# Two GpSimd waits and the low parts of one weight slot moved within a chunked gated delta rule on one Trainium2 core

## The chip, the cores and the metric

The kernel runs on one core of one Trainium2 chip. The metric is the device time of one execution in microseconds (us), taken as the median over several executions. Five engines work side by side and meet at semaphores: TensorE (PE in the profile, its weight loads as PEld), VectorE (DVE), ScalarE (ACT), GpSimd (POOL) and SyncE (SP), which only issues DMAs here. Each engine runs its own instructions strictly in the order in which they stand. TensorE writes to the accumulator memory PSUM, in eight banks that the kernel hands out in rotation.

## The reference

Two transformer blocks run one after the other on 256 tokens of width 1024. The first is a hybrid of neighbourhood attention and a gated delta rule, each over eight heads of 64; the second has two layers of feed-forward, token mixing, gating and feed-forward. The change lies inside the delta rule of the first block:

```python
def _gdn_chunked(q, k, v, g, beta, s0):
    gc = jnp.cumsum(g, axis=-1)
    decay = jnp.exp(jnp.where(incl, gc[..., :, None] - gc[..., None, :], -jnp.inf))
    kb = k * beta[..., None]
    lower = jnp.where(strict, jnp.einsum('bnhid,bnhjd->bnhij', kb, k) * decay, 0.0)
    a_mat = lower + jnp.eye(C, dtype=f32)
    rhs = jnp.concatenate([v * beta[..., None], kb * jnp.exp(gc)[..., None]], axis=-1)
    sol = lax.linalg.triangular_solve(a_mat, rhs, left_side=True, lower=True, unit_diagonal=True)
    ...
    def step(S, xs):
        v_new = u_i - jnp.einsum('bhck,bhkv->bhcv', w_i, S)
        o_i = jnp.einsum('bhck,bhkv->bhcv', qd_i, S) + jnp.einsum('bhij,bhjv->bhiv', qk_i, v_new)
        S = S * gt_i[..., None, None] + jnp.einsum('bhck,bhcv->bhkv', kd_i, v_new)
        return S, o_i
```

It runs forward and backward over context and latent tokens. After it come the neighbourhood attention, the merge of both branches, and the second block, whose output is returned. All of it is in float32. The kernel gets that precision out of rounded matmuls by splitting each weight in a rounded high part and the low part that is left, and each activation likewise, and summing three products.

## The kernel before, in words

**Weights.** Weights stream from HBM in slots of 128x2048 into a ring of four. For each split slot ScalarE makes the high part in two halves (`head`, recorded at line 1341) and VectorE subtracts it for the low part, in two halves of 128x1024 (`part`, recorded at line 1792; both its operands lie in SBUF, in `ring` and `w_hi_first`). Each half raises `w_lo_done` by one. The first block has SPLIT_1 = 25 split slots, numbered 0 to 24. The last eight of them carry the weights of four gate blocks, two slots each: slots 23 and 24 belong to the last, `g1_3`. TensorE's `gate_blocks` does eight steps for each, of six products of 128x512; steps 0 to 3 use slot 23 and steps 4 to 7 use slot 24.

**The delta rule.** The 512 tokens are four tiles of 128, and a round n = 0 to 3 handles one tile in each direction d = 0, 1. One round is this ladder:

- `lower(n)` (VectorE): the strictly triangular matrix of a round, products out of PSUM times the decays `Et`. This is read one round ahead: round 0's loop does `lower(1)`. Four instructions, which empty four PSUM banks that TensorE wants back.
- `coefficients(n)` and `invert(n)` (VectorE): shuffles, then a 16x16 inverse by elimination, 30 small products and subtractions, each waiting for the one ahead of it. All are of the tile `cst` with two operands in SBUF.
- `spread(n)` (VectorE): lays the small inverses out for TensorE, four products and two transposes. The transposes raise the semaphore `X32`, by two in a round, to eight after round 3. They are the "first-level inverses", at line 2050.
- first, second and last level (TensorE, with ScalarE copies and `first_level(n)` of VectorE between them): the inverse grows from 16 to 32, 64 and 128.
- `VN`, `SU`, `PO` (TensorE): new values, state update, output. `VN` needs the right side `R` (VectorE, line 1786) and the last copies of the inverse by ScalarE (line 1562).
- `state(n)` (VectorE): the state `sblk` is scaled and added to. In round 0 it is a copy.

In round 0, TensorE puts the gate block `g1_3` between the levels: two steps, first level out, two steps, second level in, two steps, second level out, two steps, then the queries' transposes (line 418).

**GpSimd** works down one list. `mul` of it is recorded at line 1248:

- `scaled(n)`: for each direction `gm`, of 128x1024, which TensorE's `decays(n)` reads, and `kb`, of 128x512, which its `scaled_keys(n)` reads. The title calls these the coefficients.
- `decayed_keys(n)`: two products of 128x512.
- `masked_decays(n)`: two of 128x1024 on `Et`, which VectorE's `KQ` products read in rounds 2 and 3.
- the bias masks: two of 128x2048 on `ring` (line 1305), which the attention reads.

Its second DMA of `x_in` stands between `decayed_keys(2)` and `masked_decays(3)`.

**What sets the order.** The program is written out by hand for each engine. There is no scheduler. PSUM banks rotate in TensorE's order of opening: `open_bank` waits until the group eight openings earlier was read out. So the first-level output of round 0 (`Z4`) waits for the first two instructions of `lower(1)`, and `KQ` of direction 1 in round 3 for the two `QS` groups that VectorE reads after `R`.

Of the kernel before, what the change touches and what calls it, by code (L numbers as in the profile page):

```python
# [73 lines left out]
SPLIT_1 = 6 + 1 + 18  # L74
# [5 lines left out]
def build(nc, stream, const, const_2, par1, par2, ln_params, rpb_bands, x_in, ctx_in, positions, out):  # L80
# [8 lines left out]
    with ctx:  # L89
# [5 lines left out]
        def S(name):  # L95

            if name not in sems:
                sems[name] = ctx.enter_context(nc.semaphore(name))
            return sems[name]
# [76 lines left out]
        X32 = [carve(Z + 13312 + 768 * d, 2, 8, 32) for d in range(2)]  # L176
# [198 lines left out]
        def lo_sem(j):  # L375
            return S("w_lo_done"), 2 * j
# [864 lines left out]
        @block.gpsimd  # L1241
        def _(pool):
            pool.dma_start(xtok, x_in.rearrange("(t p) f -> p t f", p=P)).then_inc(S("x_in"), 16)
            pool.dma_start(ctxtok, ctx_in.rearrange("(t p) f -> p t f", p=P)).then_inc(S("ctx_in"), 16)
            pool.dma_start(cst[:, 0:CONST_FIRST], const).then_inc(S("const_in"), 16)
            pool.dma_start(pos_i[:, :], positions).then_inc(S("pos_in"), 16)
            pool.wait_ge(S("const_in"), 16)
            mul = lambda o, a, b: nc.gpsimd.tensor_tensor(o, a, b, ALU.mult)
            pool.wait_ge(S("g_ready"), 1)
            pool.wait_ge(S("qk_ready"), 1)  # L1250
            pool.wait_ge(S("beta"), 1)
            pool.wait_ge(S("na_ready"), 1)
            summed(pool, ("dnz", 1))
            def keys(t):
                return dntok[:, t, 512:1024].rearrange("p (h e) -> p h e", e=64)

            def scaled(n):
                for d in range(2):
                    t = ORDER[d][n]
                    if n:  # L1260
                        for half in range(2):
                            summed(pool, ("Et", n - 1, d, half))
                        summed(pool, ("kbT", n - 1, d))
                    mask = K("lower") if d == 0 else K("upper")
                    mul(gm[d][:, :, :], lg[:, t, d * 8:d * 8 + 8].unsqueeze(2).to_broadcast([P, 8, P]),
                        mask.unsqueeze(1).to_broadcast([P, 8, P])).then_inc(S("gm"), 1)
                    mul(kb[d].rearrange("p (h e) -> p h e", e=64), keys(t),
                        beta[:, t, d * 8:d * 8 + 8].unsqueeze(2).to_broadcast([P, 8, 64])).then_inc(S("kb"), 1)

            def decayed_keys(n):  # L1270
                for d in range(2):
                    t = ORDER[d][n]
                    if n:
                        summed(pool, ("SU", n - 1, d))
                    mul(kdec[d].rearrange("p (h e) -> p h e", e=64), keys(t),
                        egc[:, t, 16 + d * 8:24 + d * 8].unsqueeze(2).to_broadcast([P, 8, 64])).then_inc(S("kdec"), 1)

            def masked_decays(n):
                for d in range(2):
                    for half in range(2):  # L1280
                        moved(pool, ("KK", n, d, half))
                    incl = K("upper_incl") if d == 0 else K("lower_incl")
                    mul(Et[n % 2][d], Et[n % 2][d], incl.unsqueeze(1).to_broadcast([P, 8, P])).then_inc(S("Etm"), 1)

            scaled(0)
            scaled(1)
            pool.wait_ge(S("X32"), 2)
            scaled(2)
            moved(pool, "gc")
            summed(pool, ("g1_3", 1))  # L1290
            for d in range(2):
                nc.gpsimd.memset(Xt[d], 0.0).then_inc(S("zeros"), 1)
            decayed_keys(0)
            scaled(3)
            decayed_keys(1)
            masked_decays(2)
            decayed_keys(2)
            for d in range(2):
                summed(pool, ("Y6", 2, d))
            pool.dma_start(xtok, x_in.rearrange("(t p) f -> p t f", p=P)).then_inc(S("x_in"), 16)  # L1300
            masked_decays(3)
            pool.wait_ge(S("bias_in"), 16 * 4)
            for t in range(2):
                b64 = bias[t].rearrange("p h (y c) -> p (h y) c", c=64)
                nc.gpsimd.tensor_tensor(b64, b64, K("na_mask").unsqueeze(1).to_broadcast([P, 32, 64]), ALU.add)\
                    .then_inc(S("bias"), 1)

            def ln_load(L, which):

                pool.dma_start(lnp, ln_params[L, (which - 1) * 2 * D:which * 2 * D].rearrange("(a b) -> a b", b=D)  # L1310
                               .partition_broadcast(P)).then_inc(S("ln_in"), 16)

            for L in range(LAYERS):
                if L:
                    pool.wait_ge(S(f"x{L}0"), 2)
                else:
                    pool.wait_ge(S("x00"), 4)
                    pool.dma_start(cst[:, CONST_COMMON:CONST_COLS], const_2).then_inc(S("const2_in"), 16)
                pool.dma_start(pr2, par2[L, :, :]).then_inc(S(f"par{L}_in"), 16)
                ln_load(L, 1)  # L1320
                for which in (1, 2):
                    pool.wait_ge(S(f"x{L}{which}"), 2)
                    ln_load(L, which + 1)
# [448 lines left out]
        def _(dve):  # L1772
# [18 lines left out]
            def sub(o, a, b):  # L1791
                return V_.tensor_tensor(o, a, b, ALU.subtract)  # L1792
# [40 lines left out]
            def part(upto):  # L1833

                while parted[0] < upto:
                    j = parted[0]
                    at = SPLIT_SLOTS[j] % RING * SLOT
                    hi, lo = parts(j)
                    for i in range(2):
                        h = slice(i * SLOT // 2, (i + 1) * SLOT // 2)  # L1840
                        dve.wait_ge(S("w_hi_done"), 2 * j + i + 1)
                        sub(lo[:, h], ring[:, at + h.start:at + h.stop], hi[:, h].bitcast(f32))\
                            .then_inc(S("w_lo_done"), 1)
                    parted[0] += 1
# [247 lines left out]
            part(23)  # L2092
            invert(0)
            spread(0)
            part(SPLIT_1)
            for n in range(4):
                if n:
                    state(n - 1)
                if n < 3:
                    lower(n + 1)  # L2100
                first_level(n)
                if n < 3:
                    coefficients(n + 1)
                if n == 0:
                    invert(n + 1)
                    summed(dve, ("g1_3", 1))
                for d in range(2):
                    t = ORDER[d][n]
                    v = heads(dntok[:, t, 1024:1536])
                    R = heads(Rr[d])  # L2110
                    bt = wide(beta[:, t, d * 8:d * 8 + 8], 64)
                    cum = wide(egc[:, t, d * 8:d * 8 + 8], 64)
                    if n:
                        ps, free = take(dve, ("KS", n, d))
                        mul(R, heads(ps), cum).then_inc(free, 1)
                        moved(dve, ("KS", n, d))
                        link(sub(R, v, R))
                        mul(R, R, bt).then_inc(S("R"), 1)
                    else:
                        mul(R, v, bt).then_inc(S("R"), 1)  # L2120
                for d in range(2):
                    t = ORDER[d][n]
                    cum = wide(egc[:, t, d * 8:d * 8 + 8], 64)
                    if t < 2:
                        ps, free = take(dve, ("QS", n, d))
                        if n == 2:
                            mul(heads(odn[:, t, :]), heads(ps), cum).then_inc(free, 1)
                        else:
                            mul(heads(dtmp), heads(ps), cum).then_inc(free, 1)
                            moved(dve, ("QS", n, d))  # L2130
                            link(add(odn[:, t, :], odn[:, t, :], dtmp))
                for d in range(2):
                    if ORDER[d][n] < 2:
                        dve.wait_ge(S("Etm"), 2 * (n - 2) + d + 1)
                        halves("KQ", n, d, lambda h, ps: mul(Et[n % 2][d][:, h, :], Et[n % 2][d][:, h, :], ps), True)
                if n in (1, 2):
                    invert(n + 1)
                if n < 3:
                    spread(n + 1)
# [515 lines left out]
```

## Time and profile before

| | |
|---|---|
| median of 3 runs | 1771.11 us (1769.55 to 1786.57) |
| the profiled execution | 1768.32 us |
| its span, first to last instruction | 1766.5 us |
| TensorE busy | 1690.6 us, 96% |
| VectorE busy | 1087.7 us, 62% |
| ScalarE busy | 832.1 us, 47% |
| GpSimd busy | 62.3 us, 4% |
| DMA | 285.75 MB, 162 GB/s |
| TensorE on the chain that ended last | 85% of the span |

All times on the timeline are counted from the first instruction of the profiled execution. TensorE's instructions are pipelined, so a busy time is not a time at its peak; its idle times are exact to a few tenths. The profile puts each idle time down to the instruction whose semaphore came last. The granted clock is a share of full speed: 1.00 is 2.4 GHz and 0.50 is 1.2 GHz.

### The profile page before, as it was taken

To read this page: it belongs to the slowest core of one execution; us is meant where nothing else is said; L and a number is where in the kernel's file an instruction comes from. 1 tells how busy PE (TensorE), PEld (TensorE's weight loads), DVE (VectorE), ACT (ScalarE), POOL (GpSimd) and SP (SyncE) were. 2 spreads that over 40 slices of the span, in tenths; PEclk is the share of its full clock that TensorE was granted. 3 is DMA by queue.
4 is the path that set the end of the run, shared out by engine and by line. 5 is a ranking of instruction groups with operands and counts; after the bars stand their busy time and mean duration, and the time that the engine had idled before them with its cause. 6 is when DMAs were issued, how large, how long until landed. Compare 5 with 4: busy or idle time off the path is not lost.

```text
span 1766.5 us, 24089 instructions
## 1 busy us (share of the span) xinstructions
PE 1690.6 (96%) x9832; PEld 1369.1 (78%) x9832; DVE 1087.7 (62%) x1602; ACT 832.1 (47%) x1224; POOL 62.3 (4%) x48
## 2 busy tenths in 40 slices
PE   7999989778999999999999999999999999999998
PEld 2778877677558887887888888788887878888886
DVE  3689576976236556655786554655556547875555
ACT  3444565534135444454645444444435546454442
POOL 0000133020000000000000000000000000000000
PEclk9999998887999999999999999999999999999999
DMA  8333421010365555543445555565555534455553
GB/s 350 143 122 118 167 73 26 4 72 1 143 235 185 188 191 191 190 168 119 167 167 214 191 180 183 203 216 190 183 176 206 174 140 147 164 217 191 178 182 117
DMA packets 41518, 285.75 MB, mean 162 GB/s; under 512 B 4416, under 2 KB 6592, under 8 KB 8000
## 3 DMA queue, kind: packets, MB, share of 16 engines
q1 hardware_dynamic: 39120, 268.61, 42.9%
q0 software_dynamic: 2288, 15.60, 2.3%
q8 instruction: 79, 1.29, 0.3%
q14 instruction: 31, 0.25, 0.0%
HBM read 283.14 MB, written 1.05 MB: 161 GB/s over the span
## 4 chain that ended last, share of the span: by engine, by line
PE 85%; DVE 7%; ACT 3%; DMA 2%; issue 2%; SPq 0%; POOL 0%; DVEq 0%; ACTq 0%; POOLq 0%
PE psum L415 82%; PE psum L418 3%; DMA ring<-stream 2%; DVE ring_lo L1792 2%; DVE cst L1786 1%; DVE arena L1786 1%; ACT arena L1341 1%; ACT cst L1341 1%; DMA arena<-stream 1%; ACT w_hi L1341 1%; DVE cst L1792 0%; DVE cst L2017 0%; ACT L1607 0%; DVE arena L2251 0%; DVE sblk L1855 0%
## 5 line engine op out<-in xcount | busy, mean ns | idle before, releaser
L1792 DVE TENSOR_TENSOR ring_lo<-ring,w_hi 128x1024 fp32r<-128x1024 f32 x416 | 489.1, 1222 | 237.4 <-ACT w_hi L1341 236.1
L1341 ACT ACTIVATE w_hi<-ring 128x1024 fp32r<-128x1024 f32 x416 | 415.4, 1053 | 296.8 <-DMA ring<-stream 228.5
L415 PE MATMUL psum<-w_hi,xT_hi 128*128 128x512 f32 (+1 forms) x1184 | 465.9, 393 | 12.9 <-DVE xT_lo L1792 12.2
L415 PE MATMUL psum<-w_hi,xT_lo 128*128 128x512 f32 (+1 forms) x1184 | 460.7, 389 | 0.0
L415 PE MATMUL psum<-ring_lo,xT_hi 128*128 128x512 f32 (+1 forms) x1184 | 460.6, 389 | 0.0
L415 PEld LDWEIGHTS psum<-w_hi,xT_hi 128*128 128x128 f32 x1184 | 224.2, 189 | 58.9 <-issue 14.8
L415 PEld LDWEIGHTS psum<-w_hi,xT_lo 128*128 128x128 f32 x1184 | 224.2, 189 | 46.2
L415 PEld LDWEIGHTS psum<-ring_lo,xT_hi 128*128 128x128 f32 x1184 | 224.2, 189 | 43.6
L1786 DVE TENSOR_TENSOR arena<-psum,arena 128x256 f32<-128x256 f32 (+1 forms) x144 | 73.9, 520 | 175.3 <-ACT arena L1618 124.3
L1341 ACT ACTIVATE arena<-psum 128x512 f32<-128x512 f32 (+6 forms) x165 | 87.0, 556 | 199.0 <-PE psum L415 141.5
L415 PE MATMUL psum<-arena 32*32 32x32 f32 (+7 forms) x2088 | 144.9, 259 | 33.5 <-ACT arena L1562 7.0
L415 PEld LDWEIGHTS psum<-arena 32*32 32x32 f32 (+3 forms) x2088 | 130.4, 161 | 48.3 <-issue 34.1
L415 PE MATMUL psum<-w_hi,hfT_hi 128*128 128x512 f32 x352 | 137.9, 392 | 0.0
L415 PE MATMUL psum<-w_hi,hfT_lo 128*128 128x512 f32 x352 | 137.2, 390 | 0.0
L415 PE MATMUL psum<-ring_lo,hfT_hi 128*128 128x512 f32 x352 | 137.2, 390 | 0.0
L1618 ACT ACTIVATE arena<-psum 128x256 f32<-128x256 f32 x88 | 33.7, 384 | 167.2 <-PE psum L415 167.2
L418 PE MATMUL psum<-cst,arena 128*128 128x128 f32 (+1 forms) x676 | 96.4, 279 | 4.3 <-ACT arena L1586 1.7
L418 PEld LDWEIGHTS psum<-cst,arena 128*128 128x128 f32 (+1 forms) x676 | 80.8, 143 | 22.7 <-issue 5.9
L1792 DVE TENSOR_TENSOR ring_lo<-ring,w_hi_first 128x1024 fp32r<-128x1024 f32 x50 | 65.1, 1348 | 21.8 <-ACT w_hi_first L1341 21.7
L415 PEld LDWEIGHTS psum<-w_hi,hfT_lo 128*128 128x128 f32 x352 | 66.1, 188 | 13.7
L415 PEld LDWEIGHTS psum<-w_hi,hfT_hi 128*128 128x128 f32 x352 | 66.1, 188 | 13.5
L415 PEld LDWEIGHTS psum<-ring_lo,hfT_hi 128*128 128x128 f32 x352 | 66.1, 188 | 13.5
(245 smaller groups left out, 1819.8 us busy)
## 6 DMA issues: line engine op xcount, KB each, us to landing
ring<-stream SPq DMA_DIRECT2D x249, 1024.0 KB, 4.8
arena<-ln_params POOLq DMA_DIRECT2D x6, 1024.0 KB, 5.8
arena<-par POOLq DMA_DIRECT2D x2, 1858.0 KB, 9.5
arena<-stream SPq DMA_DIRECT2D x3, 1024.0 KB, 6.9
arena<-x_in POOLq DMA_DIRECT2D x2, 1024.0 KB, 9.1
ring<-rpb_bands SPq DMA_DIRECT2D x4, 512.0 KB, 6.1
cst<-const POOLq DMA_DIRECT2D x1, 1728.0 KB, 7.6
arena<-ctx_in POOLq DMA_DIRECT2D x1, 1024.0 KB, 19.3
```

Of the source, the lines that this page charges most:

```text
L415: owe(nc.tensor.matmul(o, lhsT, rhs, start=first, stop=last), sem)
L418: owe(nc.tensor.transpose(o, i, ident), sem)
L1341: return A(o, i, ACT.Copy)
L1618: A(hs[:, cb % 2, t, :], ps[:, 0:256], ACT.Silu).then_inc(S(f"silu{L}{f}"), 1)
L1786: return V_.tensor_tensor(o, a, b, ALU.mult)
L1792: return V_.tensor_tensor(o, a, b, ALU.subtract)
```

## The change

Three edits. GpSimd's `scaled(2)` waits for `w_lo_done` at 48, which is both halves of slot 23, in place of `X32` at 2. Its `masked_decays(3)`, and with it the bias masks that follow, waits in addition for `X32` at 8, the end of `spread(3)`. VectorE makes only slot 23's low parts after `spread(0)`; those of slot 24 stand behind `first_level(0)`, ahead of `coefficients(1)`.

```diff
@@ gpsimd
             scaled(0)
             scaled(1)
-            pool.wait_ge(S("X32"), 2)
+            lo, count = lo_sem(23)
+            pool.wait_ge(lo, count + 2)
             scaled(2)
             moved(pool, "gc")
             summed(pool, ("g1_3", 1))
@@ gpsimd
             for d in range(2):
                 summed(pool, ("Y6", 2, d))
             pool.dma_start(xtok, x_in.rearrange("(t p) f -> p t f", p=P)).then_inc(S("x_in"), 16)
+            pool.wait_ge(S("X32"), 8)
             masked_decays(3)
             pool.wait_ge(S("bias_in"), 16 * 4)
@@ vector
             part(23)
             invert(0)
             spread(0)
-            part(SPLIT_1)
+            part(SPLIT_1 - 1)
             for n in range(4):
                 if n:
                     state(n - 1)
                 if n < 3:
                     lower(n + 1)
                 first_level(n)
+                part(SPLIT_1)
                 if n < 3:
                     coefficients(n + 1)
```

VectorE at the end of `spread(0)`, before. The second row is the transposes of `spread(0)`, `ring_lo` rows are low parts of a slot (two halves each; the buffer numbered 54 holds slot 23, the one numbered 56 slot 24), `ring<-psum,arena` is `lower(1)`, `arena<-arena,psum` and the transposes behind it are `first_level(0)`, and the last row opens `coefficients(1)`.

```order
L1786 TENSOR_TENSOR arena<-cst 128x256 x4
L2050 STREAM_TRANSPOSE arena<-arena 128x256 x2
L1792 TENSOR_TENSOR ring_lo<-ring,w_hi_first_54 128x1024 x2
L1792 TENSOR_TENSOR ring_lo<-ring,w_hi_first_56 128x1024 x2
L1786 TENSOR_TENSOR ring<-psum,arena 128x4x128 x4
L1792 TENSOR_TENSOR arena<-arena,psum 128x256 x2
L2062 STREAM_TRANSPOSE arena<-arena 128x256 x2
L2005 STREAM_TRANSPOSE cst<-cst 128x256 x2
```

The same place of the changed kernel, whose lines of VectorE have numbers two higher:

```order
L1788 TENSOR_TENSOR arena<-cst 128x256 x4
L2052 STREAM_TRANSPOSE arena<-arena 128x256 x2
L1794 TENSOR_TENSOR ring_lo<-ring,w_hi_first_54 128x1024 x2
L1788 TENSOR_TENSOR ring<-psum,arena 128x4x128 x4
L1794 TENSOR_TENSOR arena<-arena,psum 128x256 x2
L2064 STREAM_TRANSPOSE arena<-arena 128x256 x2
L1794 TENSOR_TENSOR ring_lo<-ring,w_hi_first_56 128x1024 x2
L2007 STREAM_TRANSPOSE cst<-cst 128x256 x2
```

The two subtractions of slot 24 moved past `lower(1)` and `first_level(0)`, six instructions and two transposes.

GpSimd from `decayed_keys(2)` to the bias masks, before: two products of keys, the DMA of `x_in`, `masked_decays(3)`, and the masks at line 1305.

```order
L1248 TENSOR_TENSOR arena<-arena,small 128x512 [waits bank1_full]
L1248 TENSOR_TENSOR arena<-arena,small 128x512 [waits bank2_full]
L1300 DMA arena<-x_in 128x2x1024 [waits bank0_full,bank7_full]
L1248 TENSOR_TENSOR arena<-arena,cst 128x1024 [waits bank6_empty,bank5_empty]
L1248 TENSOR_TENSOR arena<-arena,cst 128x1024 [waits bank0_empty,bank7_empty]
L1305 TENSOR_TENSOR ring<-ring,cst 128x2048 [waits bias_in]
L1305 TENSOR_TENSOR ring<-ring,cst 128x2048
```

And in the changed kernel:

```order
L1248 TENSOR_TENSOR arena<-arena,small 128x512 [waits bank1_full]
L1248 TENSOR_TENSOR arena<-arena,small 128x512 [waits bank2_full]
L1301 DMA arena<-x_in 128x2x1024 [waits bank0_full,bank7_full]
L1248 TENSOR_TENSOR arena<-arena,cst 128x1024 [waits bank6_empty,bank5_empty,X32]
L1248 TENSOR_TENSOR arena<-arena,cst 128x1024 [waits bank0_empty,bank7_empty]
L1307 TENSOR_TENSOR ring<-ring,cst 128x2048 [waits bias_in]
L1307 TENSOR_TENSOR ring<-ring,cst 128x2048
```

No row moved here; the fourth gained the wait for `X32`, and three stand behind it.

## Rows read from the trace of the kernel before

**Rows 1.** Windows of the span: busy us (instructions) by engine, granted clock, DMA share, GB/s.

```profile
250.00:392.00 142.00, 109.83 (x2479) 100.31 (x2481) 117.88 (x266) 67.74 (x152) 42.09 (x23) 0.83 0.11 26
...
512.00:1766.50 1254.50, 1230.29 (x5730) 1018.56 (x5728) 756.75 (x964) 599.19 (x816) 4.54 (x9) 0.99 0.51 182
```

**Rows 2.** Whom TensorE waited for between 252 and 400 us: total, times, longest.

```profile
PE psum L415 <- DVE arena L2050: 6.5, 2, 6.2
PE psum L415 <- DVE ring L1786: 5.9, 1, 5.9
```

**Rows 3.** Timeline of GpSimd: start, us, instruction, count, idle before and its releaser.

```profile
252.52 2.94 POOL L1248 TENSOR_TENSOR arena<-small,cst 128x1024 f32<-128x1024 f32 x1 [26.54 <-DVE arena L2050]
...
279.26 2.49 POOL L1248 TENSOR_TENSOR arena<-arena,small 128x512 f32<-128x512 f32 x2
285.98 1.89 POOL L1248 TENSOR_TENSOR arena<-small,cst 128x1024 f32<-128x1024 f32 x1 [4.23 <-PE psum L418]
287.83 1.04 POOL L1248 TENSOR_TENSOR arena<-arena,small 128x512 f32<-128x512 f32 x1
...
351.11 0.77 POOL L1300 DMA_DIRECT2D arena<-x_in  x1 [21.96 <-PE psum L415]
351.90 4.66 POOL L1248 TENSOR_TENSOR arena<-arena,cst 128x1024 f32<-128x1024 f32 x2
356.52 7.58 POOL L1305 TENSOR_TENSOR ring<-ring,cst 128x2048 f32<-128x2048 f32 x2
```

**Rows 4.** Timeline of VectorE, from an earlier slot's low parts to round 0's end.

```profile
217.23 2.36 DVE L1792 TENSOR_TENSOR ring_lo<-ring,w_hi_first 128x1024 fp32r<-128x1024 f32 x2 [0.69 <-ACT w_hi_first L1341]
...
252.48 8.88 DVE L1792 TENSOR_TENSOR ring_lo<-ring,w_hi_first 128x1024 fp32r<-128x1024 f32 x4
261.28 2.47 DVE L1786 TENSOR_TENSOR ring<-psum,arena 128x512 f32<-128x512 f32 x4
...
266.18 0.77 DVE L2005 STREAM_TRANSPOSE cst<-cst 128x256 f32<-128x256 f32 x2 [0.16 <-ACT cst L1341]
...
270.60 0.29 DVE L2023 COPY cst<-cst 128x256 f32<-128x256 f32 x1
...
279.68 2.62 DVE L1786 TENSOR_TENSOR arena<-arena,small 128x512 f32<-128x512 f32 x2
```

**Rows 5.** Timeline of TensorE around the gate block and the first `VN`.

```profile
262.70 0.27 PE L415 MATMUL psum<-arena 32*32 32x32 f32 x3 [5.87 <-DVE ring L1786]
...
277.34 1.34 PE L418 MATMUL psum<-cst,arena 128*128 128x128 f32 x8
...
289.50 1.30 PE L415 MATMUL psum<-arena 128*128 128x64 f32 x5 [3.26 <-ACT arena L1562]
```

**Rows 6.** Windows of low granted clock, columns as in rows 1.

```profile
262.00:269.00 7.00, 6.30 (x139) 5.33 (x140) 5.97 (x17) 4.98 (x12) 0.26 (x1) 0.51 0.01 2
290.00:300.00 10.00, 10.00 (x64) 9.88 (x67) 4.37 (x8) 2.16 (x4) 3.13 (x3) 0.52 0.01 2
```

**Rows 7.** Timeline of VectorE around the last inverse and the state of round 2.

```profile
351.40 12.80 DVE L1786 TENSOR_TENSOR cst<-cst 128x52 f32<-128x52 f32 x1
364.24 0.25 DVE L1792 TENSOR_TENSOR cst<-cst 128x52 f32<-128x52 f32 x1
...
373.74 0.42 DVE L1786 TENSOR_TENSOR sblk<-sblk,small 64x256 f32<-64x256 f32 x1
...
378.04 0.69 DVE L1789 TENSOR_TENSOR arena<-arena,psum 128x512 f32<-128x512 f32 x1
...
381.10 0.69 DVE L1786 TENSOR_TENSOR arena<-psum,small 128x512 f32<-128x512 f32 x1 [0.60 <-PE psum L415]
...
386.66 0.69 DVE L1786 TENSOR_TENSOR arena<-psum,small 128x512 f32<-128x512 f32 x1
```

**Rows 8.** Timeline of TensorE at the last first level and its last `KQ`.

```profile
373.76 0.47 PE L415 MATMUL psum<-arena 32*32 32x32 f32 x17 [6.24 <-DVE arena L2050]
...
387.49 0.72 PE L415 MATMUL psum<-arena 64*128 64x128 f32 x8 [0.53 <-DVE arena L1786]
```

## The prediction

> **What bounds the kernel now.** I read the windows first, to see where TensorE is not the bound. From 512 us on it is busy 1230.29 of 1254.50 us with the clock at 0.99 [rows 1]: nothing before that stretch can change it, except its start. From 250 to 392 us it is busy for only 109.83 of 142 us, at a mean clock of 0.83, while VectorE is busy for 117.88 and the DMAs for 11% [rows 1]. That is the delta rule, and all three edits lie in it. A time won there moves the rest forward unless a wait inside the delta rule takes it back. Then I read whom TensorE waits for there. Two single waits belong to the edits: 5.87 us for `lower(1)` at 262.70 and 6.24 us for `spread(3)` at 373.76 [rows 2, 5, 8]. Last come the timelines of GpSimd and VectorE, to see why those two are late.
>
> Both are late in the same way. A half of low parts takes 1.18 us with GpSimd at rest (2.36 for two [rows 4]), but the four at 252.48 take 8.88, 2.22 each, while `scaled(2)` runs beside them [rows 3, 4]. GpSimd's first product there takes 2.94 against 1.89 for the same product at 285.98 [rows 3]. The two take turns, one instruction each. At 351.40 it is worse: a product of `invert(3)` of a kind that takes 0.25 us takes 12.80, and ends when GpSimd's four products, 4.66 + 7.58 = 12.24 us, are done [rows 3, 7]. `lower(1)`, which reads one operand from PSUM, keeps 2.47 us for four though GpSimd is still busy for its first microsecond [rows 3, 4]. So I take it that only VectorE's instructions with two SBUF operands are held.
>
> **Site A, the two edits around `scaled(2)`.** Now slot 23's low parts run alone, 252.48 to 254.84, and `lower(1)` follows to 257.31; its first two instructions, all that TensorE's `Z4` needs, are out by 256.1. TensorE is then still in its gate steps until 256.83 (262.70 less 5.87 [rows 5]), so the wait of 5.87 goes whole. The clock falls with it: after that wait TensorE ran at 0.51 for 7 us with 6.30 busy [rows 6]. At full clock this is some 3.2 us less. No pause of such length stands ahead of it any more, so the queries' transposes at 277.34 [rows 5] come 9.0 us sooner, at 268.3.
>
> Is slot 24 late for TensorE? `Z4` starts at 256.8, and `first_level(0)`, done 3.3 us after `Z4`'s start before (to 266.0, the start of the next row less its wait [rows 4, 5]), is done 2.7 us after it at full clock, at 259.5. `scaled(2)`, 5.86 us alone (twice 1.89 + 1.04 [rows 3]), runs from 254.85 and meets the two halves at its end: they take 3.4 us in place of 2.36, to 262.95, the first by 260.8 to 261.8. TensorE wants them at about 261.4 and 265.3 (eight gate steps and the levels between them, at the full-clock pace). Cost 0 to 0.4 us; I take 0.
>
> Who is late next? `VN` of round 0, at 289.50, waited 3.26 us for ScalarE [rows 5], whose chain starts at the gate block's end and therefore moves by 9.0 too, to 280.5. It also needs `R`. VectorE: 262.95, plus 4.42 for `coefficients(1)` (266.18 to 270.60), plus 9.08 for `invert(1)` (to 279.68 [rows 4]), is 276.45. Before, `invert(1)` had GpSimd beside it only in a memset. Now GpSimd's `decayed_keys(0)`, two products of 1.04, come at 279.26 − 9.0 = 270.3, into the middle of it, and hold it for 2.1: 278.55. And `scaled(3)` comes at 285.98 − 9.0 = 277.0 [rows 3], with 1.5 us of `invert(1)` left, of which 0.8 is three or four two-operand steps. Each lets one GpSimd product by: 5.86 us and four steps of 0.2 bring it to 283.6, two transposes 0.7, the first `R` 0.65: 285.0. So `VN` starts at 285.0, not 280.5, and of the 9.0 us **4.5 remain**. The bounds are 4.5 (all four steps held) and 9.0 (`invert(1)` finds its end before `scaled(3)`; `R` then waits once, to 279.6, in time). I take the lower because all four steps fall within 0.8 us, though a microsecond either way decides it. `spread(1)` stands behind `R` and is ready ten microseconds ahead of TensorE.
>
> **Site B, the masks behind `X32` at 8.** `invert(3)` loses its 12.5 us, save up to 0.2 beside the DMA issue at 351.11 [rows 3, 7]. `spread(3)` ends at 351.7 + (373.74 − 364.24) = 361.2 [rows 7] in the old time, and TensorE, whose own work runs until 367.5 (373.76 less 6.24 [rows 8]), no longer waits. The 12.24 us of GpSimd work now start at 361.3, beside `state(2)`. This has four products with two SBUF operands (`sblk` and `small`). By turns they let the four GpSimd products by: the last ends at 361.3 + 12.24 + 3 × 0.42 + 0.42 = 375.2, and with one addition of 0.42 and one of 0.69 `state(2)` is done at 376.3. Before, it was 378.73 [rows 7]. That is 2.4 us. The 0.34 and 0.60 us that VectorE waited for TensorE behind it go too, since TensorE has done its levels meanwhile. The last reader that TensorE's `KQ` waits for at 387.49, the product at 386.66 [rows 7, 8], thus comes 3.3 us sooner. **I take 3.3.** The ladder behind is TensorE's and ScalarE's, and moves along. The bounds: 1.1, if the first state product is held through all four, as at 351.40 (361.3 + 12.24 + 5.0 for `state(2)` is 378.5; the 0.94 of waits goes); and 5.5, if VectorE is ahead of GpSimd at each turn and the last mask falls behind `state(2)`. The readers of `masked_decays(3)` stand behind the product at 386.66 in VectorE's order [rows 7], those of the masks behind them, and 375 is well ahead of that: nothing.
>
> The Trainium skill, page "SBUF — State Buffer", section "Who interferes with whom", says that a VectorE instruction with two SBUF inputs contends with a GpSimd instruction that reads SBUF, and that whoever issues first has the port for that whole instruction. By that rule one VectorE instruction waits for one of GpSimd's: the 8.88 agrees, and site B gives 3.3. The 12.80 of one instruction beside four does not agree; by it site B gives 1.1.
>
> **The sum.** 1768.32 − 4.5 − 3.3 = 1760.5 us for a run like the profiled one. This stood 2.8 us under the median of the three, so the forecast is **1763 us**.
>
> **The rivals.**
> - *No collision at A* (`invert(1)` ends before `scaled(3)`): 9.0 + 3.3, so 1759. For it: the margin is 1.5 us of a chain that I added up over 26. Chance 0.25.
> - *Held through at B*: 4.5 + 1.1, so 1765. For it: the one long case in the trace, and the same four instructions. Against: at 252.48 they took turns, and at 351.40 a DMA issue of GpSimd was under way. Chance 0.15.
> - *All of it and more*: 9.0 + 5.5, and half of the clock's other low stretches in the delta rule, another 3 to 4: 1753. Chance 0.07.
> - *The change does not reach its wait*: TensorE waits for slot 24 instead of slot 23. The price is at most the 0.4 to 1 us above; the bulk would still go. Chance 0.03, 1764.
> - *Slower.* The pause ahead of the first `VN` grows from 3.26 us to 7.8. After the pause of before, the clock was at 0.52 through 290 to 300 [rows 6], where TensorE was fully busy. If the longer pause drags the low clock through the rest of the round and on into round 1, another 16 us of TensorE's work at half clock costs 8 and eats the gain; 20 cost 10: 1768.32 − 7.8 + 10, with 2.8, is 1773. It decides once low stretches of the delta rule grow by over 16 us in all. For it: the pauses of 5.87 and 3.26 us were both followed by such stretches [rows 5, 6]. Against: one long pause and one low stretch go. Chance 0.05.
>
> The forecast itself has 0.45. **The range** is 1754 to 1771: it holds the first three cases with their bounds and a microsecond or two of run to run; left out are most of the case of 1753 and the slower one. About 1% (18 us) is what counts as a change here. Faster by over 1%, under 1753.4: 0.07. Within 1%: 0.90. Slower by over 1%: 0.03.
>
> **What would show it.** Low parts at 252.48 of 2.36 us for two, and `Z4` at 256.8 with no wait: site A's first half. `VN` of round 0 waiting for VectorE's line of `R` at 285, not for ScalarE at 280.5: the collision; single steps of `invert(1)` of over 1 us beside it. Steps of `invert(3)` all of 0.25; `spread(3)`'s wait gone from TensorE's list; products of `sblk` of 2 to 4 us each (turns), or one of 12. From 512 us on all rows alike, shifted. I am wrong if the queries' transposes move by under 7 us, if `VN` starts within a microsecond of 289.50, or if TensorE's rows behind 512 us lengthen.

## The result

| | before | changed |
|---|---|---|
| median | 1773.32 us (18 runs) | 1760.89 us (18 runs) |
| lowest to highest | 1765.13 to 1786.57 | 1755.76 to 1770.48 |
| profiled execution | 1768.32 us | 1760.34 us |

The ratio is 0.9941, 95% interval 0.9921 to 0.9961: the change makes the kernel faster by 10 us, 7 to 14. A second set of 12 runs gave 0.9939 (0.9916 to 0.9962). The forecast was 1763, in a range of 1754 to 1771.

The windows of the changed kernel, with the borders moved along with the work (columns as in [rows 1]):

```profile
250.00:380.00 130.00, 105.88 (x2460) 96.13 (x2459) 112.86 (x272) 68.25 (x152) 38.79 (x23) 0.87 0.12 27
...
500.00:1758.50 1258.50, 1234.28 (x5727) 1021.14 (x5725) 756.32 (x964) 599.24 (x816) 4.22 (x8) 0.99 0.52 181
```

The border is 12 us earlier because TensorE's last `KQ` comes 11.7 us earlier (375.76 below, 387.49 in [rows 8]). So the delta rule is 12 us shorter, and the rest is 4 us longer; the last section puts that down to the clock. TensorE's waits between 250 and 392 us, to lay beside [rows 2]:

```profile
PE psum L415 <- DVE arena L1788: 8.4, 3, 5.2
PE psum L415 <- ACT arena L1564: 7.0, 4, 3.3
...
PE psum L415 <- DVE arena L2052: 0.3, 1, 0.3
```

The 5.9 us for `lower(1)` are gone from the list and the 6.2 us for `spread(3)` shrank to nothing (the 0.3 are round 0's). A new one of 2.3 us is inside the first line. TensorE's own rows in the changed kernel: its first first-level product of round 0, the start of `Z4`, the second half of `Z4`, the queries' transposes, `VN` of round 0, `VN` of round 2, the last `KQ`, `VN` of round 3.

```profile
254.03 0.36 PE L415 MATMUL psum<-arena 32*32 32x32 f32 x20 [0.29 <-DVE arena L2052]
...
258.31 0.26 PE L415 MATMUL psum<-arena 32*32 32x32 f32 x8
...
259.69 0.18 PE L415 MATMUL psum<-cst,arena 32*32 32x32 f32 x1 [0.64 <-issue]
...
271.20 0.44 PE L418 MATMUL psum<-cst,arena 128*128 128x128 f32 x2
...
283.36 0.41 PE L415 MATMUL psum<-arena 128*128 128x64 f32 x2 [3.26 <-ACT arena L1564]
...
347.69 6.56 PE L415 MATMUL psum<-arena 128*128 128x64 f32 x39 [1.90 <-ACT arena L1564]
...
375.76 0.38 PE L415 MATMUL psum<-arena 64*128 64x128 f32 x2 [2.29 <-DVE arena L1788]
...
383.46 2.75 PE L415 MATMUL psum<-arena 128*128 128x64 f32 x23 [0.82 <-ACT arena L1564]
```

And two of the same places in the kernel before, the first first-level product of round 0 and `VN` of round 2 (the others are in [rows 5, 8]; `VN` of round 3 started at 394.39):

```profile
252.50 1.29 PE L415 MATMUL psum<-arena 32*32 32x32 f32 x128 [0.30 <-DVE arena L2050]
...
355.15 2.08 PE L415 MATMUL psum<-arena 128*128 128x64 f32 x17 [1.90 <-ACT arena L1562]
```

Round 0 began 1.5 us later here than in the trace of before (254.03 against 252.50, ahead of all edits), so I compare intervals. From the first first-level product to `VN` of round 0 it is 29.3 us, where it was 37.0 (289.50 less 252.50). The last `KQ` still waits for VectorE, as [rows 8] had it, but longer: 2.29 us in place of 0.53.

### The profile page after: what moved, and what is told of

Same layout as the page of the kernel before. It is cut to its first block, busy times and chain, and to the rows that moved or that the text cites. A ratio compares the mean times of both kernels' runs of the same rounds, so it can differ in the third digit from the quotient of the medians.

```text
span 1758.5 us, 24089 instructions
## 1 busy us (share of the span) xinstructions
PE 1692.0 (96%) x9832; PEld 1367.2 (78%) x9832; DVE 1081.2 (61%) x1602; ACT 832.6 (47%) x1224; POOL 59.0 (3%) x48
## 3 DMA queue, kind: packets, MB, share of 16 engines
q8 instruction: 79, 1.29, 0.3%
## 4 chain that ended last, share of the span: by engine, by line
PE 87%; DVE 6%; ACT 3%; DMA 2%; issue 1%; SPq 0%; POOL 0%; DVEq 0%; ACTq 0%; POOLq 0%
PE psum L415 84%; PE psum L418 3%; DMA ring<-stream 1%; DVE ring_lo L1794 1%; ACT arena L1343 1%; DVE arena L1788 1%; DVE sblk L1788 1%; ACT cst L1343 1%; DMA arena<-stream 1%; ACT w_hi L1343 1%; DVE cst L2019 0%; ACT L1609 0%; DVE arena L2254 0%; DVE sblk L1857 0%; DVE cst L1794 0%
## 5 line engine op out<-in xcount | busy, mean ns | idle before, releaser
L415 PE MATMUL psum<-arena 32*32 32x32 f32 (+7 forms) x2088 | 141.1, 252 | 23.4 <-DVE arena L1788 8.4
L415 PEld LDWEIGHTS psum<-arena 32*32 32x32 f32 (+3 forms) x2088 | 126.7, 154 | 38.1 <-issue 30.4
L1794 DVE TENSOR_TENSOR ring_lo<-ring,w_hi_first 128x1024 fp32r<-128x1024 f32 x50 | 61.2, 1268 | 21.5 <-ACT w_hi_first L1343 21.4
```

Of the source, the lines that this page charges most:

```text
L415: owe(nc.tensor.matmul(o, lhsT, rhs, start=first, stop=last), sem)
```

## The experiments

Two intervals tell the sites apart better than the whole time does. Site A is from the first first-level product of round 0 to `VN` of round 0. Site B is from `VN` of round 2 to `VN` of round 3. In us, from one trace each:

| kernel | site A | site B |
|---|---|---|
| before | 37.0 | 39.2 |
| changed, two traces | 29.3, 30.0 | 35.8, 35.3 |
| edits 1 and 3 | 29.7 | 40.6 |
| edit 2 | 35.9 | 35.4 |
| edit 3, two traces | 30.0, 30.0 | 39.5, 40.5 |
| edit 1 | 33.1 | 39.2 |
| idle work ahead of `invert(1)` | 35.2 | 36.5 |
| the same, `scaled(3)` behind `R` | 30.7 | 35.3 |
| masks apart, two traces | 31.4, 29.9 | 34.4, 35.6 |
| DMA behind the masks | 36.1 | 38.1 |

Rows that share the code of a site show how far a single trace can be off. Site A with its old code took 37.0, 35.9 and 36.1 us (before, edit 2, DMA behind the masks), and with its new code 29.3, 30.0, 29.7, 31.4 and 29.9: 6.3 us between the means, where the first pair of traces shows 7.7. Site B took 38.1 to 40.6 us in the six traces without edit 2, and 35.3 to 36.5 in the five with it and its masks in place: about 4 us.

### Each site alone

Site A alone (edits 1 and 3):

```diff
-            pool.wait_ge(S("X32"), 2)
+            lo, count = lo_sem(23)
+            pool.wait_ge(lo, count + 2)
...
-            part(SPLIT_1)
+            part(SPLIT_1 - 1)
...
                 first_level(n)
+                part(SPLIT_1)
```

> The first and third edit alone (scaled(2) behind slot 23's low parts, slot 24's behind first_level(0)); masked_decays(3) waits for nothing new. Theory: the two sites add up. From the first first-level product of round 0 to VN of round 0 29.3 us as in the changed kernel (37.0 before), and one product of invert(3) held for about 12 us again, with TensorE waiting 6 us for spread(3). Time 7 to 8 us under before. Rival: the sites are coupled, and most of the gain comes with the masks: under 4 us.

Site B alone (edit 2):

```diff
+            pool.wait_ge(S("X32"), 8)
             masked_decays(3)
```

> The second edit alone (masked_decays(3) and the masks behind X32 at 8). Theory: VN of round 2 to KQ of direction 1 in round 3 takes 28.1 us as in the changed kernel (32.3 before), the four sblk products are held by turns, 2 to 4 us each, and the 5.9 us wait for lower(1) stays. Time 4 us under before. Rival: without site A nothing comes of it: within 1 us.

By the intervals both expectations held. Site A took 29.7 us with edits 1 and 3, and one step of `invert(3)` was held again:

```profile
347.14 12.86 DVE L1793 TENSOR_TENSOR cst<-cst 128x56 f32<-128x56 f32 x1
```

Site B took 35.4 us with edit 2, and `VN` of round 2 to the last `KQ` 28.45 (expected 28.1); the 5.87 us wait for `lower(1)` stayed. One detail was not as expected: three of the four `sblk` products were held there (1.91, 3.50 and 2.74 us), and the fourth took 0.42, since TensorE released the first of them later. So each site keeps its own interval, whatever the code of the other. The whole times came out smaller than expected: ratio 0.9978 (0.9949 to 1.0006) for site A, some 4 us, and 0.9995 (0.9970 to 1.0020) for site B, 1 us. The intervals take in 7 and 4 us, and they take in none; the two sum to half of the 10 us of both together. That the sites are additive is read from the traces and not shown by the times.

### Which edit does site A's work

Edit 3 alone, slot 24's low parts behind `first_level(0)`:

```diff
-            part(SPLIT_1)
+            part(SPLIT_1 - 1)
...
                 first_level(n)
+                part(SPLIT_1)
```

> The third edit alone: slot 24's low parts behind first_level(0), scaled(2) still on X32 at 2, so that it runs beside slot 23's low parts. By turns these take about 4.1 us in place of 2.36, lower(1) starts 1.8 us later, and TensorE waits about 1.5 us for it ahead of Z4, in place of 5.9 before and none in the changed kernel. If the order of VectorE alone did it, the wait is gone; if the sharing alone did it, it stays near 5.

Edit 1 alone, `scaled(2)` behind slot 23:

```diff
-            pool.wait_ge(S("X32"), 2)
+            lo, count = lo_sem(23)
+            pool.wait_ge(lo, count + 2)
```

> The first edit alone: scaled(2) waits for slot 23's low parts, slot 24's still ahead of lower(1). Slot 23's take 2.36 us and slot 24's about 4.2, together 6.6 in place of 8.9, so TensorE waits 3.5 to 3.9 us for lower(1) in place of 5.9.

VectorE with edit 3 alone:

```profile
252.87 4.06 DVE L1792 TENSOR_TENSOR ring_lo<-ring,w_hi_first 128x1024 fp32r<-128x1024 f32 x2
256.86 2.47 DVE L1786 TENSOR_TENSOR ring<-psum,arena 128x512 f32<-128x512 f32 x4
```

and with edit 1 alone:

```profile
253.54 6.33 DVE L1793 TENSOR_TENSOR ring_lo<-ring,w_hi_first 128x1024 fp32r<-128x1024 f32 x4
```

Slot 23's two halves took 4.06 us beside GpSimd (expected 4.1), and all four took 6.33 where slot 23 ran alone (expected 6.6). TensorE waited 1.03 and 3.30 us for `lower(1)`. Both expectations of the wait were a little too high, by 0.5 and by 0.2 to 0.6 us. Against the first trace of before, edit 3 alone brings 7.0 of the 7.7 us of site A and edit 1 alone 3.9 (against the mean of its three traces 6.3 and 3.2): they are two ways to the same wait, and the order of VectorE is the stronger. With edit 3 in place, what edit 1 adds (30.0 to 29.3 or 30.0) is within what two traces of one kernel differ by. Edit 3 alone, timed again:

> The third edit alone, timed. By its trace it has 7.0 of site A's 7.7 us. Theory: what it lost in its single time lay behind the delta rule, where nothing of it differs, so 5 to 8 us under before. Rival: the order of VectorE has a cost elsewhere, and it is level with before or slower.

0.9951 (0.9922 to 0.9980), so 4 to 14 us faster on its own. Its first, single time of 1779.17 us had its excess behind the delta rule, as expected: from `VN` of round 3 on, that trace took 1386.3 us and the second one 1373.4.

### The collision that did not come

The prediction took 4.5 us for site A because `scaled(3)` was to hold the end of `invert(1)` and `R`. To see whether that mechanism exists, VectorE got idle work:

```diff
                 part(SPLIT_1)
+                if n == 0:
+                    for _ in range(4):
+                        link(V_.tensor_reduce(held, cst[:, 0:768], AX, ALU.add))
                 if n < 3:
                     coefficients(n + 1)
```

> The changed kernel with four idle reductions of 128x768 (one operand, 0.8 us each, nothing reads them) put on VectorE behind slot 24's low parts, about 3.5 us. This brings the collision that the prediction assumed at site A: invert(1) then has some 2 us left when scaled(3) starts. Theory of turns: four of its steps are held, one for each GpSimd product, R is late, and VN of round 0 waits for VectorE's R and starts 4 to 5 us later against the first-level products than in the changed kernel (34 us behind them in place of 29.3). Rival (no such collision exists; ScalarE bounds VN in any case): within 0.5 us of 29.3.

VectorE in it, the steps of `invert(1)` from 279.14 on:

```profile
279.14 0.25 DVE L1795 TENSOR_TENSOR cst<-cst 128x84 f32<-128x84 f32 x1
279.42 1.98 DVE L1789 TENSOR_TENSOR cst<-cst 128x72 f32<-128x72 f32 x1
281.43 0.96 DVE L1795 TENSOR_TENSOR cst<-cst 128x72 f32<-128x72 f32 x1
282.43 1.81 DVE L1789 TENSOR_TENSOR cst<-cst 128x60 f32<-128x60 f32 x1
284.27 0.96 DVE L1795 TENSOR_TENSOR cst<-cst 128x60 f32<-128x60 f32 x1
285.27 0.21 DVE L1789 TENSOR_TENSOR cst<-cst 128x48 f32<-128x48 f32 x1
```

and GpSimd beside it, `scaled(3)`:

```profile
279.41 1.90 POOL L1249 TENSOR_TENSOR arena<-small,cst 128x1024 f32<-128x1024 f32 x1 [4.64 <-PE psum L419]
281.27 1.04 POOL L1249 TENSOR_TENSOR arena<-arena,small 128x512 f32<-128x512 f32 x1
282.27 1.90 POOL L1249 TENSOR_TENSOR arena<-small,cst 128x1024 f32<-128x1024 f32 x1
284.12 1.04 POOL L1249 TENSOR_TENSOR arena<-arena,small 128x512 f32<-128x512 f32 x1
```

Read the two side by side: each of the four long steps ends as a GpSimd product ends, and the fifth takes 0.21 us again. `VN` of round 0 started 35.2 us behind the first-level products (expected 34), after a wait of 8.91 us for VectorE. Then the same with `scaled(3)` out of the way:

```diff
+            pool.wait_ge(S("R"), 2)
             scaled(3)
```

> The same four idle reductions, and scaled(3) waiting for R of round 0. If scaled(3) is what delays R in the kernel before this one, invert(1) and R run unheld, ScalarE is again what VN of round 0 waits for, and it starts 29.3 to 30 us behind the first-level products. If the reductions themselves delay it, 33 us or more as there.

No step was held by `scaled(3)`, and site A took 30.7 us. (In both kernels `decayed_keys(0)` held the first two steps of `invert(1)`, to 0.96 to 0.98 us each.) I had expected ScalarE to be what `VN` waits for, at 29.3 to 30 us; it was still VectorE, so the idle work itself cost up to 1.4 us. The other 4.5 (35.2 less 30.7) are `scaled(3)`'s. The mechanism is real, and the changed kernel escapes it by 1.3 us, from the end of the last step at 278.55 to the start of `scaled(3)` at 279.84:

```profile
278.37 0.18 DVE L1794 TENSOR_TENSOR cst<-cst 128x16 f32<-128x16 f32 x1
278.57 0.70 DVE L2035 STREAM_TRANSPOSE cst<-cst 128x128 f32<-128x128 f32 x2
279.31 2.99 DVE L1788 TENSOR_TENSOR arena<-arena,small 128x512 f32<-128x512 f32 x2
```

That is VectorE of the changed kernel: the last step of `invert(1)`, the transposes, and `R`. GpSimd beside it, `decayed_keys(0)` and the first product of `scaled(3)`:

```profile
273.12 2.12 POOL L1248 TENSOR_TENSOR arena<-arena,small 128x512 f32<-128x512 f32 x2
279.84 1.92 POOL L1248 TENSOR_TENSOR arena<-small,cst 128x1024 f32<-128x1024 f32 x1 [4.59 <-PE psum L418]
```

The second `R` product was held here (2.99 us for the two, 1.29 unheld), in time for `VN`. In all seven traces with edit 3 and without idle work, `VN` of round 0 waited 3.26 us for ScalarE, and the margin was 1.3 us once, 1.6 in five and 3.0 in one.

### Why one step was held through four products

In the kernel before, one step of `invert(3)` took 12.80 us [rows 7], though everywhere else the engines took turns. A DMA that GpSimd issues stands 0.8 us ahead of the four products. Moving it behind them:

```diff
             for d in range(2):
                 summed(pool, ("Y6", 2, d))
-            pool.dma_start(xtok, x_in.rearrange("(t p) f -> p t f", p=P)).then_inc(S("x_in"), 16)
             masked_decays(3)
...
                     .then_inc(S("bias"), 1)
+            pool.dma_start(xtok, x_in.rearrange("(t p) f -> p t f", p=P)).then_inc(S("x_in"), 16)
```

> The kernel before with GpSimd's second DMA of x_in put behind the bias masks; its wait for Y6 of round 2 stays ahead of masked_decays(3). Why is one step of invert(3) held through four GpSimd products? If the DMA issue ahead of them is what does it, the four products now hold four steps by turns, some 2.4, 2.4, 3.9 and 3.9 us. If it is anything else (these products, this step), one step of over 12 us stays. Invert(3) as a whole is 12 us late either way, and the time is that of before within noise.

VectorE's steps of `invert(3)` that took over 1.5 us, all of them:

```profile
354.18 2.44 DVE L1792 TENSOR_TENSOR cst<-cst 128x60 f32<-128x60 f32 x1
356.65 2.29 DVE L1786 TENSOR_TENSOR cst<-cst 128x56 f32<-128x56 f32 x1
358.97 3.73 DVE L1792 TENSOR_TENSOR cst<-cst 128x56 f32<-128x56 f32 x1
362.74 3.75 DVE L1786 TENSOR_TENSOR cst<-cst 128x52 f32<-128x52 f32 x1
```

Four steps by turns, in one trace, as expected if the DMA issue ahead is what made one step wait through. The case with the DMA ahead showed one step of 12.79 to 12.86 us in five traces of five (before, site A alone, edit 1 alone, edit 3 alone twice). The issue by itself holds nothing: in the seven traces in which it has no product right behind it, the steps that ran during its 0.77 us took 0.25 to 0.27. In the changed kernel, GpSimd's issue and one of these steps:

```profile
343.65 0.77 POOL L1301 DMA_DIRECT2D arena<-x_in  x1 [21.96 <-PE psum L415]
343.93 0.25 DVE L1788 TENSOR_TENSOR cst<-cst 128x52 f32<-128x52 f32 x1
```

So it is the issue with products right behind it. How the two together do it was not tried. The time lost is much the same either way: 12.55 us in the one long step, and some 11.2 in the four.

### Masks where nothing meets them

The changed kernel still lets `masked_decays(3)` and the masks hold the products of `state(2)`:

```profile
354.57 1.86 DVE L1788 TENSOR_TENSOR sblk<-sblk,small 64x256 f32<-64x256 f32 x1 [0.86 <-PE psum L415]
...
356.89 2.03 DVE L1788 TENSOR_TENSOR sblk<-sblk,small 64x256 f32<-64x256 f32 x1
...
360.13 2.74 DVE L1788 TENSOR_TENSOR sblk<-sblk,small 64x256 f32<-64x256 f32 x1
...
363.34 3.50 DVE L1788 TENSOR_TENSOR sblk<-sblk,small 64x256 f32<-64x256 f32 x1
```

GpSimd beside them:

```profile
353.80 4.84 POOL L1248 TENSOR_TENSOR arena<-arena,cst 128x1024 f32<-128x1024 f32 x2 [9.38 <-DVE arena L2052]
358.60 7.95 POOL L1307 TENSOR_TENSOR ring<-ring,cst 128x2048 f32<-128x2048 f32 x2
```

One more kernel moves both parts:

```diff
             decayed_keys(2)
+            masked_decays(3)
             for d in range(2):
                 summed(pool, ("Y6", 2, d))
             pool.dma_start(xtok, x_in.rearrange("(t p) f -> p t f", p=P)).then_inc(S("x_in"), 16)
-            pool.wait_ge(S("X32"), 8)
-            masked_decays(3)
+            for half in range(2):
+                moved(pool, ("KQ", 3, 1, half))
             pool.wait_ge(S("bias_in"), 16 * 4)
```

> The changed kernel with masked_decays(3) moved ahead of the x_in DMA, beside coefficients(3), which has one SBUF operand per instruction, and the masks behind the KQ products of round 3, where VectorE waits for TensorE for some 10 us. Theory (GpSimd holds only VectorE's instructions with two SBUF operands): the sblk products take 0.42 us each, invert(3) is held nowhere, TensorE's wait of 2.3 us ahead of the last KQ goes, VN of round 2 to that KQ takes 25 to 26 us in place of 28.1, and the time is 2 to 3 us under the changed kernel. Rival (GpSimd slows coefficients(3) too): its shuffles lengthen and nothing is won.

> The kernel with masked_decays(3) beside coefficients(3) and the masks behind the last KQ again. Theory: the first trace showed it only 0.6 us ahead up to the last KQ, because TensorE's own work there took 1.6 us longer at the low clock; so 0 to 3 us under the changed kernel, and more likely than not the intervals overlap. Rival (the turns at state(2) still cost their 2 to 3 us in the median): 3 us or more under it.

```profile
362.35 0.42 DVE L1789 TENSOR_TENSOR sblk<-sblk,small 64x256 f32<-64x256 f32 x1 [2.71 <-PE psum L415]
```

This is VectorE in the first of its two traces: every `sblk` product of `state(2)` took 0.42 us, and it waited 2.71 us for TensorE first. In round 3 nothing was held. But `VN` of round 2 to the last `KQ` took 27.5 us, not 25 to 26 (28.1 in the changed kernel), and 28.3 in the second trace: the expectation missed. TensorE reached the first level of round 3 13.9 us behind that `VN` in both traces, where it took 12.3 in the first trace of the changed kernel (and 13.9 in the second), with no wait ahead of it in any of them and 10.2 us at the low clock in place of 6.8. So its own work was the bound up to there. The second pair of traces shows no gain at site B at all (35.6 against 35.3). In time it stood at 0.9916 (0.9888 to 0.9944) and 0.9909 (0.9876 to 0.9943), with medians of 1758.45 and 1758.53 us against 1760.89 (from another set of runs) and 1760.82. It is the fastest of the kernels here both times, by some 2.4 us, but the intervals overlap with those of the changed kernel, and its traces show no place for the gain. I leave open whether it is one.

## Why the prediction was right

**Site A: the mechanism right, one term not.** The low parts of slot 23 ran alone in 2.36 us and `lower(1)` in 2.48, as worked out:

```profile
254.00 2.36 DVE L1794 TENSOR_TENSOR ring_lo<-ring,w_hi_first 128x1024 fp32r<-128x1024 f32 x2
256.28 2.48 DVE L1788 TENSOR_TENSOR ring<-psum,arena 128x512 f32<-128x512 f32 x4
```

`Z4` began at 258.31, when the gate steps ended, with no wait for VectorE. The queries' transposes came 7.7 us sooner, not 9.0. One part is that the clock gave back 2.4 us and not 3.2: I halved all of TensorE's 6.30 busy us [rows 6]. The twelve gate products behind `Z4` went from 4.9 to 3.0 us, but the 128 small products of `Z4` from 1.9 to only 1.4, without the pause between them. The other is that pause, 0.64 us of `issue` in the middle of `Z4` (259.69), a kind of wait that I had not costed; what it is stays open. The 7.7 are also on the high side: in the two other traces with the old code of site A, the twelve gate products took 3.8 and 4.0 us, and the interval up to the transposes 23.7 and 24.0 in place of 24.8.

Two errors cancelled at slot 24. `first_level(0)` was done 3.6 us behind the start of `Z4`, not 2.7, and the two halves behind it took 2.63 us, not 3.4, since `scaled(2)` was nearly done by then.

The step that failed is "who is late next". I let `scaled(3)` meet the end of `invert(1)` and took 4.5 of the 9.0 us, the lower bound, with a note that a microsecond decides. It came 1.3 us later than worked out, since TensorE gained 7.7 and not 9.0, and `invert(1)` ended 0.8 us earlier, mostly since `decayed_keys(0)` held it for 1.4 us in place of 2.1. The margin was 1.3 us, ScalarE remained what `VN` waits for with the same 3.26 us, and all of the 7.7 stayed. That is the rival with a chance of 0.25; the case that I had held most likely did not come. The experiment with idle work shows that its price was right: 4.5 us.

**Site B: right, somewhat more.** `invert(3)` ran unheld; `masked_decays(3)` and the masks started behind `spread(3)` and held the four `sblk` products by turns, one each (1.86, 2.03, 2.74, 3.50 us). The Trainium skill, page "SBUF — State Buffer", section "Who interferes with whom", has the shared port held for the whole instruction of whoever issues first; the four rows agree, each ending 0.3 us behind the end of one GpSimd instruction. (In the second trace TensorE released the first of them later, and three were held: 1.96, 3.50 and 2.75 us.) 3.3 us were expected up to the last `KQ`; the traces give 4.3 (32.34 to 28.07), of which TensorE still waits 2.29. The term that was mis-sized is GpSimd's part in the turns: I had it lose three times 0.42 us to VectorE on top of its 12.24, and it took 12.75 from first to last (353.80 to 366.55). Of the 4.3 us, 0.8 were lost again between that `KQ` and `VN` of round 3 (6.9 us before, 7.7 now), which is why the table shows 3.4. The rival of one product held through all four did not come, and the experiment with the DMA says why it is not to be expected: no DMA issue stands right ahead of them any more.

**The sum.** 7.7 and 4.3 us in the traces are 12.0; the profiled runs differ by 8.0, the medians by 12.4, and the ratio gives 10. I had 7.8. The agreement with the 8.0 of the profiled runs is an accident. 1.5 us ahead of the edits and 3.7 behind the last `KQ` went the other way, and the stretch between the sites was 1.3 us shorter, which makes 12.0 − 1.5 − 3.7 + 1.3 = 8.1. That the median fell within 2 us of the forecast is partly luck too: I took 7.8 off a median of three runs, 1771.11, and the median of 18 is 1773.32. The whole time cannot tell the forecast's 1763 from the 1759 of the rival that came; the traces can.

**The signs.** One sign of being wrong did show in this pair: TensorE's rows behind 512 us lengthened, from 1230.29 to 1234.28 us busy. It does not count against the change, since that stretch differs by up to 13 us between two executions of one kernel (last section), but it was a poor sign to choose.

**Slower** did not come: the pause ahead of `VN` stayed at 3.26 us, so its condition was not met.

## What to carry to other kernels

When two engines hold each other up, look for what each late instruction is held by, one by one. Here a VectorE product with two SBUF operands beside a GpSimd product cost as much as the GpSimd product left to run (a step of 0.23 us took 1.98), so short linked steps (an elimination) are the worst neighbours. Products with one operand in PSUM lost nothing there (`lower(1)` took 2.47 and 2.48 us beside GpSimd, before and in the changed kernel, and `lower(3)` 2.48 with GpSimd at rest). Move the GpSimd work beside those, and move VectorE's own bulk work behind what TensorE's banks wait for: the second alone had 7.0 of the 7.7 us of site A here. A transfer of the gain through four engines needs the margin of each to be known to a microsecond; where it is not, keep both outcomes in the range.

## What the runs showed that I had not expected

**The same 6224 products took 1369 to 1386 us.** From `VN` of round 3 on, TensorE has the same 6224 products in all kernels here. Windows of that stretch alone, for edit 1 alone, site B alone and edit 3 alone, one row each:

```profile
390.09:1758.80 1368.71, 1335.63 (x6224) 1085.30 (x6224) 804.20 (x1066) 637.56 (x891) 4.80 (x9) 0.99 0.49 175
```

```profile
390.31:1770.50 1380.19, 1347.35 (x6224) 1095.10 (x6224) 804.38 (x1066) 637.50 (x891) 4.80 (x9) 0.98 0.49 173
```

```profile
391.07:1777.30 1386.23, 1355.54 (x6224) 1102.09 (x6224) 804.36 (x1066) 637.27 (x891) 4.80 (x9) 0.97 0.49 172
```

VectorE's and ScalarE's busy times agree to 0.3 us; only TensorE's grow, with its granted clock lower. The rows round the clock to two digits. The stretches at 0.50 that each trace records there add up to 27, 57 and 74 us for these three, and in the other ten traces to 37 to 73 us, at 1372.1 to 1386.3 us in all: some 0.37 us more for each microsecond at the low level (17.5 for 47). It does not go by kernel: edit 3 alone took 1386.3 us in one trace and 1373.4 in the other, with 74 and 37 us at the low level. These differences are larger than the whole gain of a site, and what decides them was not found. This is why single times here (1760.68 for edit 1 alone, 1779.17 for edit 3 alone) rank the kernels wrongly, and why the intervals between marks inside a trace did the work.

**GpSimd's DMA issue changes the turns.** With it right ahead of a run of GpSimd products, one VectorE step waited through all four, 12.79 to 12.86 us; without it, four steps waited for one each. The issue with nothing behind it held no step.

**A copy with one SBUF operand was held too.** I had taken it that only instructions with two SBUF operands are. In both kernels with idle work, VectorE's copy ahead of `invert(1)` fell beside GpSimd's memset and took 0.77 and 0.82 us; in all other traces it took 0.28 to 0.30, with no GpSimd work beside it.

```profile
272.12 0.77 DVE L2026 COPY cst<-cst 128x256 f32<-128x256 f32 x1
```

Why a memset holds a copy, but not the steps of `invert(1)` beside it in the kernel before, was not tried.
